# One matmul of 256 columns made as two of 128 at 29 places in the weight streams of a transformer kernel

## The reference, cut to what is computed

```python
def swiglu(h, w_gate, w_up, w_down):
    return (jax.nn.silu(h @ w_gate) * (h @ w_up)) @ w_down
...
for layer in range(DEPTH):                  # DEPTH = 2
    h = rms_norm(x, attn_pre_g[layer])
    ...                                      # attention of the layer
    x = x + rms_norm(y, attn_post_g[layer])
    h = rms_norm(x, ffn_pre_g[layer])
    f = swiglu(h, ffn_w_gate[layer], ffn_w_up[layer], ffn_w_down[layer])
    x = x + rms_norm(f, ffn_post_g[layer])
...
    u = jnp.einsum('bsd,df->bsf', h2, w_up[l])      # third layer
    u = causal_depthwise_conv(u, w_conv[l], b_conv[l])
    u_val, u_gate = jnp.split(u, 2, axis=-1)
    y = jnp.einsum('bsf,fd->bsd', jax.nn.gelu(u_gate) * u_val, w_down[l])
```

## Time and profile before

| | us |
|---|---|
| median of three runs | 1013.06 |
| the runs | 1010.03, 1013.06, 1379.49 |
| span of the profiled execution, first to last instruction | 1000.4 |
| TensorE busy in that span | 971.1 |
| VectorE busy | 718.6 |
| ScalarE busy | 539.2 |

### The profile page before, as it was taken

How to read it: one execution, slowest core, us unless ns; L and a number is a source line. 1 busy time by engine, 2 the same in 40 slices (tenths; PEclk the granted TensorE clock), 3 DMA queues, 4 the chain that set the end, 5 groups by cost and what they waited for, 6 DMA issues and landing times.

```text
span 1000.4 us, 18847 instructions
## 1 busy us (share of the span) xinstructions
PE 971.1 (97%) x7970; PEld 935.1 (93%) x7970; DVE 718.6 (72%) x1270; ACT 539.2 (54%) x837; POOL 17.4 (2%) x48
## 2 busy tenths in 40 slices
PE   6989999999999999999999999999999999999997
PEld 6978999999998988899999998898999999999996
DVE  5965787877658777698867888556654878787843
ACT  6635564545446456565444454546755556666642
POOL 0000000000000000000000000000220000000000
PEclk9999999999999999999999999999999999999999
DMA  7533376666743833358665883543333534555531
GB/s 285 180 126 142 153 250 256 252 256 251 279 184 132 290 127 126 128 196 310 252 245 212 340 307 119 215 172 123 124 141 136 204 153 168 184 195 174 213 122 43
DMA packets 28307, 194.19 MB, mean 194 GB/s; under 512 B 3264, under 2 KB 3520, under 8 KB 5312
## 3 DMA queue, kind: packets, MB, share of 16 engines
q1 hardware_dynamic: 28224, 192.99, 52.7%
HBM read 191.93 MB, written 1.05 MB: 193 GB/s over the span
## 4 chain that ended last, share of the span: by engine, by line
PE 87%; DVE 6%; ACT 4%; issue 1%; DMA 1%; SPq 1%; POOL 0%; DVEq 0%; ACTq 0%
PE bank L492 24%; PE bank L494 24%; PE bank L493 24%; PE bank L626 2%; DVE s_wlo L1343 2%; PE bank L652 2%; PE bank L549 2%; PE bank L543 1%; PE bank L544 1%; PE bank L508 1%; ACT s_whi L885 1%; PE bank L515 1%; PE bank L509 1%; PE bank L636 1%; DMA s_raw<-in_wa 1%
## 5 line engine op out<-in xcount | busy, mean ns | idle before, releaser
L1343 DVE TENSOR_TENSOR s_wlo<-s_raw,s_whi 128x512 fp32r<-128x512 f32 (+1 forms) x364 | 371.3, 1061 | 138.4 <-ACT s_whi L885 137.9
L885 ACT ACTIVATE s_whi<-s_raw 128x1024 fp32r<-128x1024 f32 (+2 forms) x233 | 304.8, 1334 | 217.3 <-PE bank L494 204.1
L492 PE MATMUL bank<-s_hh,s_whi 128*128 128x256 f32 x1400 | 395.7, 283 | 0.4 <-DVE s_hl L1434 0.2
L493 PE MATMUL bank<-s_hl,s_whi 128*128 128x256 f32 x1400 | 390.3, 279 | 0.0
L494 PE MATMUL bank<-s_hh,s_wlo 128*128 128x256 f32 x1400 | 390.2, 279 | 0.0
L492 PEld LDWEIGHTS bank<-s_hh,s_whi 128*128 128x128 f32 x1400 | 264.9, 189 | 6.4 <-issue 5.1
L494 PEld LDWEIGHTS bank<-s_hh,s_wlo 128*128 128x128 f32 x1400 | 263.8, 188 | 0.0
L493 PEld LDWEIGHTS bank<-s_hl,s_whi 128*128 128x128 f32 x1400 | 262.9, 188 | 0.1
L494 PE MATMUL bank<-s_ph,s_wlo 128*128 128x256 f32 x528 | 146.6, 278 | 0.0
L492 PE MATMUL bank<-s_ph,s_whi 128*128 128x256 f32 x528 | 146.6, 278 | 0.0
L493 PE MATMUL bank<-s_pl,s_whi 128*128 128x256 f32 x528 | 146.6, 278 | 0.0
(11 more groups left out here) (231 smaller groups left out, 1277.5 us busy)
## 6 DMA issues: line engine op xcount, KB each, us to landing
s_raw<-in_gu SPq DMA_DIRECT2D x44, 1024.0 KB, 4.8
s_raw<-in_dn SPq DMA_DIRECT2D x33, 1024.0 KB, 4.8
s_raw<-in_wada SPq DMA_DIRECT2D x24, 1024.0 KB, 5.6
s_raw<-in_up SPq DMA_DIRECT2D x22, 1024.0 KB, 4.8
s_raw<-in_wo SPq DMA_DIRECT2D x8, 1024.0 KB, 4.8
s_raw<-in_win_g SPq DMA_DIRECT2D x8, 1024.0 KB, 4.9
s_raw<-in_wkv_v SPq DMA_DIRECT2D x4, 1024.0 KB, 5.5
s_raw<-in_wkv_k SPq DMA_DIRECT2D x4, 1024.0 KB, 4.8
```

Source lines behind the costliest of these rows:

```text
L492: e.matmul(out, hi, xh[:, k, :], start=first, stop=False, skip_group_check=True)
L493: e.matmul(out, hi, xl[:, k, :], start=False, stop=False, skip_group_check=True)
L885: e.activation(whi[w % SPLIT][:, at], raw[p % RAW][:, at], ACT.Copy).then_inc(S.hi.tick((w, c0)), 1)
L1343: e.tensor_tensor(wlo[s][:, at], raw[p % RAW][:, at], whi[s][:, at].bitcast(F32), ALU.subtract).then_inc(S.lo.tick((i, j), (i, "all")), 1)
```

## The change

At chosen places the third matmul of a `product`, low weights by high activations, is made as two: the same weight tile, columns 0 to 127 and then columns 128 to 255, into the two halves of the same output. Nothing is moved, no wait and no signal is added, and the same numbers are added up.

```diff
+HALVED = {"gu0": 8, "gu1": 8, "up2": 8, "dn0": 2, "dn1": 2, "dn2": 2, "wkv_k": 8, "win_k": 8}
...
-            def product(name, t, out, xh, xl, k, first, last, event=None):
+            def product(name, t, out, xh, xl, k, first, last, event=None, halves=False):
...
-                m = e.matmul(out, lo, xh[:, k, :], start=False, stop=last, skip_group_check=True)
+                if halves:
+                    e.matmul(out[:, 0:P], lo, xh[:, k, 0:P], start=False, stop=last, skip_group_check=True)
+                    m = e.matmul(out[:, P:T], lo, xh[:, k, P:T], start=False, stop=last, skip_group_check=True)
+                else:
+                    m = e.matmul(out, lo, xh[:, k, :], start=False, stop=last, skip_group_check=True)
...
-                                event if k == nk - 1 else None)
+                                event if k == nk - 1 else None, name in HALVED and j == 0 and k == 1 and n % HALVED[name] == 0)
...
-                                k == 0 and j == 0, k == NF - 1, (name, 0) if k == NF - 1 and j == 1 else None)
+                                k == 0 and j == 0, k == NF - 1, (name, 0) if k == NF - 1 and j == 1 else None,
+                                k == 1 and j == 0)
...
-                            k == NF - 1, ("dn2", 0) if k == NF - 1 and j == 1 else None)
+                            k == NF - 1, ("dn2", 0) if k == NF - 1 and j == 1 else None, k == 1 and j == 0)
```

## The result

The changed kernel takes 998.71 us in the median of 9 runs (998.17 to 999.14). The kernel before, run beside it, takes 1007.66 us (999.59 to 1013.06, with one run at 1379.49). The ratio is 0.9919 with a 95% interval from 0.9893 to 0.9946, so the change made the kernel 0.8% faster. That is less than the 2% bound and clear of noise all the same. The other thing to see is the scatter: 1 us over nine runs, where the kernel before has 13.

The account below looks back on a forecast made before the run. TensorE's matmul count and pace were taken to bound the kernel. Added halves cost 3.2 us against up to 10.2 us gained from the faster pace; -5 net was taken, so 1013.1 - 5 = 1008 us, range 1003 to 1022.

Parts of the forecast that it names:

- TensorE bounds the kernel, and there are two gaits: TensorE's matmul streams set the time, at a steady 0.1133 us (276 ns recorded) or 0.1178 us (281 ns) a matmul.
- The base of the sum: Whole kernel: the runs' median of 1013.1 us, 12.7 us above the profiled span of 1000.4, taken as starting time.
- the forecast of -5: Net change for the whole kernel: slow long streams caught at the first or second split, one of two single-split streams too.
- The 266 us of slow stretches: Slow matmuls behind the first split: 29 us in wkv_k and wq1, 73 gu1, 29 win_k and win_q, 135 up2 with dn2.
- The direct cost: At the 29 split places: 0.111 us for each half, 0.11 us more a place, 3.2 us in all.
- The split ends the long gait: In most slow stretches a split brings the fast pace, giving 1004 to 1012 us; chance 0.50.
- The signs named for wkv_k, gu1, win_k and dn2: Third matmul at 276 ns behind the first or second split in gu1, and in up2 and dn2 to the end.
- Rival b: A split throws fast streams (gu0, dn0, gu1, dn1, up2) into the slow pace: 9.8 us more, 1026 us; chance 0.12.
- The cover holds: Other engines keep up with faster TensorE: VectorE's 81% busy share in up2 would become 84%, nothing added for it.
- 10.2 us on offer: Gain if all slow matmuls in the split streams took the fast pace, 3.8% less time.
- What was late next: If gu1 or up2 goes faster, waits at a tile's start, with steps of 0.14 to 0.32 us, left in the range.

Follow-up runs that it names:

- again: The kernel before, run and profiled once more with nothing changed: 1006.98 us, 999.94 to 1012.49 in 12 runs.
- twin: The changed kernel, but at its 29 places the third matmul is made twice with all 256 columns instead of as two halves: 1013.34 us, ratio 1.0061.
- uneven: The changed kernel with its 29 splits made at column 192, giving 192 and then 64 columns: 1000.32 us, ratio 0.9959.
- chosen_b: Second run of the changed kernel with twelve splits chosen by name and weight tile in place of 29: 996.00 us, ratio 0.9891.

## Why the prediction was right or wrong

**TensorE bounds the kernel, and there are two gaits.** Right in gu0, wkv_k, gu1, dn1, win_k and dn2, where each matmul's step shows in the end. Wrong in up2, below.

**The base of the sum.** This step failed, and by itself it puts the time outside the range: on the 1007.66 us that the kernel before took beside the changed one, the forecast of -5 and its range would have been 1002.7 and 997.7 to 1016.7 us, which holds the measured 998.71. The prediction set the profiled execution at the median of three runs, "12.7 us above that span". The profiles with a time of their own show 2.1 us. So that execution took about 1000.4 + 2.1 = 1002.5 us (worked out, since its time is not recorded) and was one of the quicker draws of a kernel that runs from 998 to 1013 us. On that base the forecast of -5 would have been 997.5 us, and the measured span fell by 4.0. The median fell by 9 us because the typical execution of the kernel before has more of the long gait than the one that I read, as again shows. The 266 us of slow stretches, from which the gain was worked out, were that one execution's draw as well. I had seen that the gait is decided by breaks of 0.1 us and did not draw the conclusion that other executions are decided otherwise; the scatter between 1010.03 and a span of 1000.4 was the hint.

**The direct cost.** Mis-sized: 0.111 us a half, 3.2 us in all, and measured 0.127 us a place, 3.7 us if all 29 counted. The halves do not stand 0.11 us apart as expected but 0.058. The pace of one load's step for each matmul holds only over three steps, since the rest comes behind, with 0.170 us.

**The split ends the long gait.** Right, and more clearly than the 0.50 that it was given: 38 of 38 in eight profiles at the first try, where I had allowed for misses in between. In the changed kernel's own profile only 4 of 29 places met the long gait (137.7, 535.8, 871.4 and 894.0 us). The signs named for wkv_k, gu1, win_k and dn2 came true there because these streams had drawn the short gait by themselves, which was luck. The reason offered, that the stream goes by the load alone for two steps, agrees with the steps in the timeline and with twin, but uneven shows that a short matmul is not enough for itself. Why halves work wherever in the three steps they fall, and 192 with 64 columns does not, is open.

**Rival b, a split that throws the short gait into the long one.** No case in any of the profiles.

**"The cover holds."** This failed in up2. Busy shares of 81% were read as slack, but VectorE and ScalarE wait for each other in a round of 5.65 us, so the share left over could not be used. Of 10.2 us on offer, some 2.8 us (74 x 3.8%) lay in up2 and came to 0.1. In chosen_b, with one split there and only some 160 matmuls at 281 ns, it came to 0.5. That the long gait's pace and that round are both 5.65 us hid it: no wait of TensorE is on record there before.

**What was late next.** The waits at tile starts appeared, as the prediction said, in up2 and not in gu1, and took back all that was gained there. In gu1 a stretch behind the float32 sums drew the long gait (148 matmuls, 0.7 us) that the profile of before had short; that was the lottery, and the split at n = 40 ended it.

## What to carry to other kernels

Where the time of a kernel scatters by 1% from run to run at a full clock, look for stretches of like matmuls with different steps, and compare two profiles of the same program before one of them serves as a base. Before a short stretch is put down to the change, look at the steps just ahead of the changed place: the state may have been there already. Take the base from the profiled execution and the runs' own spans, never from a median and another execution's span. Before a gain in pace is credited to a stage, follow the other engines through one round, waits included: their busy share does not tell whether they can keep up.

## What was not expected of the hardware

An unbroken stream of fp32r matmuls, 128x128 weights by 256 columns and a new load for each, runs at 0.1133 or at 0.1178 us a matmul at a full granted clock, and keeps either for over 1000 matmuls. A break of 0.1 us can turn the one into the other. One matmul made as two of 128 columns four or more steps behind a break ends the long step (38 of 38 cases); two or three steps behind a break or another kind of matmul, with the first of the three matmuls split, it did so in 1 of 5. In the short step it costs 0.127 us. A whole matmul more does not end the long step (25 of 25 stayed), and a split into 192 and 64 columns does so in 5 of 9. What in the chip holds the two steps apart was not tried.
